# Sixteen latent attention heads on one core: keys projected a turn sooner and copied by halves, weights turned ahead of the next query

## What is computed

```python
cq, ckv, k_rope = jnp.split(h @ w_down, [256, 256 + 128], axis=-1)
q = (rms_norm(cq, q_norm_g) @ w_uq)      # 16 heads of 64 + 32
kv = (rms_norm(ckv, kv_norm_g) @ w_ukv)  # 16 heads of 64 keys + 64 values
...
q_rope = apply_axial_rope(q_rope, *rope)
k_rope = apply_axial_rope(k_rope, *rope)
...
s = (jnp.einsum("bqhd,bkhd->bhqk", q_nope, k_nope)
     + jnp.einsum("bqhr,bkr->bhqk", q_rope, k_rope)).astype(jnp.float32) * scale
p = jax.nn.softmax(s, axis=-1)
return jnp.einsum("bhqk,bkhe->bqhe", p.astype(v.dtype), v)
```

## Time and profile before

| | |
|---|---|
| three runs | 2318.94, 2324.66, 2324.82 us; median 2324.66 us |
| the profiled execution, its own time | 2318.96 us |
| its span in the profile | 2317.1 us (1.9 us lie around it) |
| PE busy, of the span | 2124.6 us, 92% |
| DVE, ACT, POOL busy | 1500.3, 1039.8, 7.2 us |

### The profile page before, as it was taken

The page is one execution under the profiler, slowest core; times in us unless marked ns, Lnnn a source line. Parts: engine busy times, 40 slices in busy tenths (PEclk is TensorE's granted clock), DMA queues, the critical chain, the costliest instruction groups (busy, mean ns, idle before and its releaser), DMA issues.

```text
span 2317.1 us, 33662 instructions
## 1 busy us (share of the span) xinstructions
PE 2124.6 (92%) x12966; PEld 1849.5 (80%) x12966; DVE 1500.3 (65%) x2165; ACT 1039.8 (45%) x1740; POOL 7.2 (0%) x30
## 2 busy tenths in 40 slices
PE   5989999998999889999987889997899889999997
PEld 2677888885777768888866679996899787799997
DVE  3358676686666577767777767885766654555554
ACT  4325223235566552322335655554544563444444
POOL 0000000000000000000000000000000000000000
PEclk8999999998999999999988999998999987799998
DMA  9634464442111136458551037671455531355551
GB/s 352 234 116 141 145 206 144 155 136 78 55 55 55 60 141 199 141 189 274 189 134 55 28 119 244 233 238 58 143 185 181 154 109 45 102 173 177 177 179 58
DMA packets 254192, 339.27 MB, mean 146 GB/s; under 512 B 23943, under 2 KB 232162, under 8 KB 254066
## 3 DMA queue, kind: packets, MB, share of 16 engines
q1 hardware_dynamic: 254066, 337.54, 44.2%
HBM read 336.47 MB, written 1.05 MB: 146 GB/s over the span
## 4 chain that ended last, share of the span: by engine, by line
PE 86%; DVE 6%; ACT 5%; issue 2%; DMA 1%; SPq 1%; POOL 0%; DVEq 0%; ACTq 0%
PE bank L1350 26%; PE bank L1351 25%; PE bank L1352 25%; PE bank L1968 4%; DMA mod_raw<-in_mod_w 1%; DVE norm L2048 1%; PE bank L1400 1%; PE bank L1573 1%; PE bank L1412 1%; SPq L530 0%; PE bank L1426 0%; PE bank L1890 0%; PE bank L1891 0%; ACT norm L813 0%; DVE mpt_lo L2506 0%
## 5 line engine op out<-in xcount | busy, mean ns | idle before, releaser
L1350 PE MATMUL bank<-h_hi,w_hi 128*128 128x256 f32 (+3 forms) x2024 | 673.1, 333 | 53.4 <-DVE h_lo L2057 48.6
L781 ACT ACTIVATE w_hi<-w_raw 128x1024 fp32r<-128x1024 f32 x443 | 464.8, 1053 | 525.6 <-PE bank L1352 505.1
L1351 PE MATMUL bank<-h_lo,w_hi 128*128 128x256 f32 (+3 forms) x2024 | 666.4, 329 | 0.0
L1352 PE MATMUL bank<-h_hi,w_lo 128*128 128x256 f32 (+3 forms) x2024 | 665.6, 329 | 0.0
L2024 DVE TENSOR_TENSOR w_lo<-w_raw,w_hi 128x1024 fp32r<-128x1024 f32 x443 | 539.7, 1222 | 172.1 <-ACT w_hi L781 169.6
L1350 PEld LDWEIGHTS bank<-h_hi,w_hi 128*128 128x128 f32 (+1 forms) x2024 | 392.1, 194 | 99.7 <-issue 59.3
L1352 PEld LDWEIGHTS bank<-h_hi,w_lo 128*128 128x128 f32 (+1 forms) x2024 | 391.8, 194 | 32.3
L1351 PEld LDWEIGHTS bank<-h_lo,w_hi 128*128 128x128 f32 (+1 forms) x2024 | 392.4, 194 | 31.0 <-issue 0.2
L1350 PE MATMUL bank<-g_hi,w_hi 128*128 128x512 f32 (+1 forms) x1152 | 391.1, 339 | 4.5 <-DVE g_lo L2341 3.0
L1351 PE MATMUL bank<-g_lo,w_hi 128*128 128x512 f32 (+1 forms) x1152 | 388.4, 337 | 0.0
L1352 PE MATMUL bank<-g_hi,w_lo 128*128 128x512 f32 (+1 forms) x1152 | 388.2, 337 | 0.0
(11 more groups left out here) (356 smaller groups left out, 2363.0 us busy)
## 6 DMA issues: line engine op xcount, KB each, us to landing
w_raw<-in_mlp_w SPq DMA_DIRECT2D x128, 1024.0 KB, 5.7
mod_raw<-in_mod_w SPq DMA_DIRECT2D x128, 768.0 KB, 5.2
w_raw<-in_w_expert_gate SPq DMA_DIRECT2D x16, 1024.0 KB, 5.2
w_raw<-in_w_expert_up SPq DMA_DIRECT2D x16, 1024.0 KB, 5.2
w_raw<-in_w_expert_down SPq DMA_DIRECT2D x16, 1024.0 KB, 4.9
w_raw<-in_diff_w_qkv SPq DMA_DIRECT2D x12, 1024.0 KB, 5.2
w_raw<-in_fourier_w SPq DMA_DIRECT2D x8, 1024.0 KB, 8.3
w_raw<-in_w_in SPq DMA_DIRECT2D x8, 1024.0 KB, 5.8
```

The lines of the kernel that those rows point to most:

```text
L781: act.activation(W_hi[n % RING][:, :].rearrange("p (k c) -> p k c", c=P), w_raw[slot][:, :, place, :], ACT.Copy).then_inc(s("w_hi"), 1)
L1350: pe.matmul(dst, w_hi, r_hi, start=start, stop=False)
L1351: pe.matmul(dst, w_hi, r_lo, start=False, stop=False)
L1352: return pe.matmul(dst, w_lo, r_hi, start=False, stop=stop)
```

## The change

Semaphores, counts and arithmetic stay; what changes is order, one pair of buffers, and one engine.

1. **Opening.** DVE turns the rotary key ahead of the `ckv` norm instead of behind it; ACT copies it ahead of its next panel; the two subtractions to `mk_lo` go from DVE to POOL, between its two column swaps. The sum for the `ckv` norm is issued in the middle of `cq`'s first tile instead of behind it. `query_sum` is issued ahead of `query(0)`; the `q_table` norm goes ahead of `ckv_lo` and the last panel of the opening.
2. **Keys.** `keys` of the next pair moves from odd turn t to even turn t-1, and one half is copied and subtracted in each turn, ahead of the turned weights.
3. **Turned weights.** On PE `turn_weights(t-1)` goes from behind `weighted_values(t-2)` to right behind `scores(t)`, ahead of `query(t+1)`. `mpt_hi` and `mpt_lo` are double, and ACT's copy waits for the product of two heads before instead of one. On ACT norm1 goes ahead of the copies.

```diff
-        if turn % 2:
-            add("k", (turn + 1) // 2, "mla_k_lo", turn + 3)
+        if turn % 2 == 0 and turn // 2 + 1 < MLA_HEADS // 2:
+            add("k", turn // 2 + 1, "mla_k_lo", turn + 4)
...
-        mpt_hi, mpt_lo = sb("mpt_hi", [P, 4, LAT], F32R), sb("mpt_lo", [P, 4, LAT], F32R)
+        mpt_hi = [sb("mpt_hi0", [P, 4, LAT], F32R), sb("mpt_hi1", [P, 4, LAT], F32R, over=at["norm0"])]
+        mpt_lo = [sb("mpt_lo0", [P, 4, LAT], F32R), sb("mpt_lo1", [P, 4, LAT], F32R, over=at["norm2"])]
...
             swap_rotary(u, 0)
+            pool.wait_ge(s("kr_hi"), 1)
+            pool.wait_ge(s("uq_swapped"), 1)
+            pool.tensor_tensor(mk_lo[0][HALF:P, :], kr_f[HALF:P, :], mk_hi[0][HALF:P, :].bitcast(F32),
+                               ALU.subtract).then_inc(s("kr_lo"), 1)
+            pool.tensor_tensor(mk_lo[1][0:HALF, :], kr_f[0:HALF, :], mk_hi[1][0:HALF, :].bitcast(F32),
+                               ALU.subtract).then_inc(s("kr_lo"), 1)
+            pool.wait_ge(s("kr_lo"), 2)
             swap_rotary(u + 2, 1)
...
                     if turn + 1 < MLA_HEADS:
                         query(turn + 1)
+                    if turn // 2 + 1 < MLA_HEADS // 2:
+                        keys(turn // 2 + 1, turn % 2)
+                    if on:
+                        act.wait_ge(s("z_inv"), BEFORE_MLA["z_inv"] + turn + 1)
+                        act.activation(mp_raw[turn % 2][1][:, :], mp_raw[turn % 2][1][:, :], ACT.Identity,
+                                       scale=m_zinv[:, turn % 2, 1:2]).then_inc(s("mla_norm1"), 1)
                     if 1 <= turn <= MLA_HEADS:
                         for i in range(2):
                             done, ps = attention_tile("mla", "turn_p", turn - 1, i)
                             act.wait_ge(s("aux_done"), done)
-                            if turn >= 2:
-
-                                act.wait_ge(s("pv_done"), turn - 1)
-                            act.activation(mpt_hi[:, 2 * i:2 * i + 2, :].rearrange("p a b -> p (a b)"), ps[:, :],
+                            if turn >= 3:
+
+                                act.wait_ge(s("pv_done"), turn - 2)
+                            act.activation(mpt_hi[(turn - 1) % 2][:, 2 * i:2 * i + 2, :].rearrange("p a b -> p (a b)"), ps[:, :],
                                            ACT.Copy).then_inc(s("pt_hi"), 1)
-                    if turn % 2 and turn + 1 < MLA_HEADS:
-                        keys((turn + 1) // 2)
                     for i in VALUE_TILES.get(turn, []):
                         values(i)
-                    if on:
-                        act.wait_ge(s("z_inv"), BEFORE_MLA["z_inv"] + turn + 1)
-                        act.activation(mp_raw[turn % 2][1][:, :], mp_raw[turn % 2][1][:, :], ACT.Identity,
-                                       scale=m_zinv[:, turn % 2, 1:2]).then_inc(s("mla_norm1"), 1)
...
+                query_sum()
                 query(0)
-                query_sum()
                 keys(0)
                 for turn in range(MLA_HEADS):
                     scores(turn)
+                    if turn:
+                        turn_weights(turn - 1)
                     if turn + 1 < MLA_HEADS:
                         query(turn + 1)
+                    if turn % 2 == 0 and turn // 2 + 1 < MLA_HEADS // 2:
+                        keys(turn // 2 + 1)
                     if turn >= 2:
                         weighted_values(turn - 2)
-                    if turn:
-                        turn_weights(turn - 1)
-                    if turn % 2 and turn + 1 < MLA_HEADS:
-                        keys((turn + 1) // 2)
                     for i in VALUE_TILES.get(turn, []):
                         values(i)
```

More of the change, by code:

```diff
@@ L1073, in down_outputs @@
                                scale=1.0 / KV_RANK).then_inc(s("down_root"), 1)
+                act.wait_ge(s("kr_turned"), 3)
+                act.activation(mk_hi[0][HALF:P, :], kr_f[HALF:P, :], ACT.Copy)
+                act.activation(mk_hi[1][0:HALF, :], kr_f[0:HALF, :], ACT.Copy).then_inc(s("kr_hi"), 1)
                 act.wait_ge(s("uq_swapped"), 1)
@@ L1101, in query, with keys @@
                     act.activation(mq_hi[:, :], mq_f[:, :], ACT.Copy).then_inc(s("qk_hi"), 1)
-                def keys(pair):
+                def keys(pair, j):
                     ps = made("k", pair)
-                    for j in range(2):
-                        half = slice(j * HALF, (j + 1) * HALF)
-                        act.activation(mk_hi[j][half, :], ps[half, :], ACT.Copy).then_inc(s("mla_k_hi"), 1)
+                    half = slice(j * HALF, (j + 1) * HALF)
+                    act.activation(mk_hi[j][half, :], ps[half, :], ACT.Copy).then_inc(s("mla_k_hi"), 1)
                 def values(i):
@@ L1114, in mla_attention @@
                 query(0)
-                keys(0)
+                for j in range(2):
+                    keys(0, j)
                 for turn in range(MLA_HEADS + 2):
@@ L2459, in query_lo, with keys @@
                     dve.tensor_tensor(mq_lo[:, :], mq_f[:, :], mq_hi[:, :].bitcast(F32), ALU.subtract).then_inc(s("qk_lo"), 1)
-                def keys(pair):
+                def keys(pair, j):
                     ps = made("k", pair)
-                    for j in range(2):
-                        half = slice(j * HALF, (j + 1) * HALF)
-                        dve.wait_ge(s("mla_k_hi"), 2 * pair + j + 1)
-                        dve.tensor_tensor(mk_lo[j][half, :], ps[half, :], mk_hi[j][half, :].bitcast(F32),
-                                          ALU.subtract).then_inc(s("mla_k_lo"), 1)
+                    half = slice(j * HALF, (j + 1) * HALF)
+                    dve.wait_ge(s("mla_k_hi"), 2 * pair + j + 1)
+                    dve.tensor_tensor(mk_lo[j][half, :], ps[half, :], mk_hi[j][half, :].bitcast(F32),
+                                      ALU.subtract).then_inc(s("mla_k_lo"), 1)
                 def values(i):
@@ L2505, in mla_attention @@
                             dve.wait_ge(s("pt_hi"), BEFORE_MLA["pt_hi"] + 2 * (turn - 1) + i + 1)
[L2506 to L2510 removed]
+                            hi = mpt_hi[(turn - 1) % 2][:, 2 * i:2 * i + 2, :].rearrange("p a b -> p (a b)")
+                            lo = mpt_lo[(turn - 1) % 2][:, 2 * i:2 * i + 2, :].rearrange("p a b -> p (a b)")
+                            dve.tensor_tensor(lo, ps[:, :], hi.bitcast(F32), ALU.subtract).then_inc(s("pt_lo"), 1)
                     for i in VALUE_TILES.get(turn, []):
```

50 lines of the change are left out of this document (20 added, 30 removed).

## The result

The median of five runs went from 2322.16 to 2338.26 us; the ratio is 1.0069 with a 95% interval of 1.0053 to 1.0085. That is slower by more than the 0.3% that a measurement of this kernel can tell.

What follows compares the result with a forecast made beforehand. No engine is full; a loop of waits passing between engines bounds the turns. Opening -3.6, turn 0 +0.6, turns +9.1, end +0.6 and clock +6.7 give +13.4 on 2324.66, so 2338 us; range 2324 to 2348.

Steps and rivals of the forecast that it cites:

- the ring: Attention turns: waits from row maxima through T1, query, mk_hi, norm1 and mpt_lo to the next maxima; 7.15 us, +9.1 overall.
- the clock: Turns 1 to 15: stretches at the lower clock and what they push cost 6.7 us, as in the old order; bounds 0 and 14.
- the opening: Ahead of the first scores: -1.44 sum, -4.18 rotary, +0.9 cq root, +1.1 keys; -3.6 us, between -5.6 and -1.9.
- the end: Behind turn 15's maxima: norm1 ahead of the last copies adds 0.6 us.
- Even or odd alike: Attention turns: each turn takes 7.15 us, with 7.05 as lower bound, whether even or odd.
- the sign that the maxima would stand 7.1 to 7.8 us apart: Turns 10 to 14, trace after: expected distance between row maxima, even and odd; 6 us apart would show the forecast wrong.
- the upper bound: Turns wholly at 1.2 GHz: query spacing doubles, 8.4 us, and PE's work arrives later in six even turns, 6; together 14.
- Turn 0: First attention turn: one more half of keys on ACT adds 0.6 us.
- The faster one: Turns and opening: the keys' waits go and no loop of waits replaces them; -13.8 us to 2310.9; chance 0.10.
- No change: Turns of 7.05 us at full clock throughout, opening gaining 5.6; +3.3 us, 2328; chance 0.14 for all within 7 us.
- T1's waits of 2.23 and 1.04 us: PE in the old order: T1 already waits with the query ahead of it; cited against the faster rival, chance 0.10.
- The low clock on the ring: Turns wholly at the lower clock, costing 14 us instead of 6.7; +21 us, 2345; chance 0.16.

Runs made afterwards that it cites:

- experiment 1: The changed kernel with the next head's query put back ahead of the turned weights on PE; 2318.21 us, ratio 0.9987 to the kernel before.
- 8: The changed kernel with only the second tile of the turned weights (T1) moved behind the query, the first staying ahead; 2317.91 us, ratio 0.9983 to before.
- 3: The kernel before with only the turned weights moved ahead of the query, and the double buffers; 2337.29 us, ratio 1.0063.
- experiment 9: The changed kernel with the six products of each query (heads 1 to 15) issued twice; 2345.29 us, ratio 1.0096 to the kernel before.
- 10: The changed kernel with each query's products issued twice and the query put back ahead of the turned weights; 2315.17 us, ratio 0.9968 to before.
- Experiment 11: The changed kernel with the four transposes of T0 issued three times each turn, in PE's wait ahead of T1; 2331.05 us, ratio 1.0035 to before.
- experiment 12: The changed kernel with one mpt_hi and one mpt_lo instead of two; 2342.62 us, ratio 1.0087 to the kernel before.
- experiment 4: The kernel before with only the keys' part: projected in even turns, one half copied and subtracted each turn; 2313.82 us, ratio 0.9973.
- 7: The kernel before with the change's opening and keys' parts, nothing of the turned weights' part, single buffers; 2311.8 us, ratio 0.9955.
- 5: The changed kernel with the query put back ahead of the turned weights and norm1 behind the copies to mpt_hi; 2315.96 us, ratio 0.9975 to before.

## Why the prediction was right, point by point

The mechanism was the one that was forecast. The closeness of the number, 2338 against 2338.26, is luck: the median of before that I started from was 2.5 us higher than the one measured beside the change, and the change that I added was 2.7 us too small (13.4 against 16.1). Inside it the ring and the clock were together 5 us too small, the opening and the end together 1.8 too dear.

- **The new ring.** Right, and shown from three sides: cut by putting the query back ahead of T (experiment 1) or ahead of T1 alone (8), -20 us each; closed by that one move in the kernel before (3), +16.5; lengthened by a known 0.72 us, which arrives whole in each turn (9), and hardly at all off the ring (10). I gave its length as 7.15 us for even and odd turns alike. It is 6.99 and 7.62. The even turn's links, from the rows above: 0.73, 0.83, 0.41, 1.00, 0.78, 0.48, 0.61, 0.61, 1.21, 0.33, sum 6.99; I was 0.08 low at the query and 0.1 high at each copy of ACT. "Even or odd alike" was the error, and so was the sign that the maxima would stand 7.1 to 7.8 us apart in turns 10 to 14: in the odd turn five links are longer, 0.90, 0.62, 0.74, 1.32, 0.46 against 0.78, 0.48, 0.61, 1.21, 0.33. I had taken these five links from an even turn and from the opening, or as whole durations. Turn 12, at 8.46 us, lay outside the 7.8 by the clock. Experiment 11 puts the ring with its panels and values at 111.75 us where I had 108.7, +12.2 instead of +9.1.
- **The clock.** I took +6.7, the old order's figure, with bounds 0 and 14; it was 8.5 (experiment 11). That the two are near each other was not worked out from the new order. The mechanism of the upper bound shows in turn 12: the query's products stand 0.21 us apart there instead of 0.12 (1353.25 to 1353.46).
- **The opening.** -4.7 instead of -3.6, within my bounds. Up to the `ckv` reciprocal it is -1.6 (from `mix2`'s: 23.18 us against 24.77), for which I had -1.44. From there to the `cq` reciprocal 6.06 instead of 11.90, -5.8, where I had -4.18 + 0.9: I had left out that the panel and `ckv_lo` go behind that reciprocal too. From there to the scores +2.7 (7.47 against 4.78), where I had +1.1: that same work comes back. The first scores stand at 1244.44, not near 1239.6 as I had said; 6.0 of that are the later `mix2` of this execution. POOL's subtractions cost nothing, as said; they take 1.3 us each.
- **Turn 0 and the end.** +0.7 and -0.1 for +0.6 and +0.6. The last norm1 found room.
- **The rivals.** The faster one needed a ring under 5.98 us; it is 6.99. "No change" needed full clock throughout: experiment 11 shows that case, and it still lies 0.35% above before. Against it I had named T1's waits of 2.23 and 1.04 us "with the query ahead of it"; the second is of turn 15, which has no next query, so only the first says that. The low clock on the ring was priced right in kind, 8.5 of 14 us. The second buffer is needed in the new order alone, and is worth about 4 us there (experiment 12); the fastest kernel has single buffers.
- **One judgement failed beside the forecast:** I treated the keys' move as a mere redistribution. It gains 7.5 us by itself (experiment 4), and with the opening it would have made a faster kernel (7).

Stays open: why the point ahead of the attention lies up to 6 us later in some executions; I compared stretches to be free of it. The medians aren't: in experiment 9 they give 7.0 us where the stretches give 10.6.

## What to carry to other kernels

Before an instruction is moved on an engine that works in order, ask of the instruction that it is put behind what that one waits for. A product that feeds a long chain (here the query) must not stand behind one that waits for a buffer of a shared ring to be read in the same round; walk once round the loop of waits and add it up, odd and even rounds apart. A change of several parts should be timed in parts: here two of three gained 10 us together, and one move took 20. PE's idle time isn't free either where the granted clock falls behind it: a wait filled with useless work made this kernel 7 us faster, and turn 4 with useful work in that place took 5.87 us instead of 8.44 (experiments 7 and 5).
